# Seven block products in place of eight in the up projections of three feed-forwards

## The reference

```python
n = rmsnorm(h, P['norm_g'][l, 0]) * (1 + sc0) + s0
h = h + 0.5 * g0 * swiglu(n, P['w_ffn_up'][l, 0], P['w_ffn_down'][l, 0])
...
def swiglu(x, w_up, w_down):
    g, u = jnp.split(x @ w_up, 2, axis=-1)
    return (jax.nn.silu(g) * u) @ w_down
```

## Time and profile before

| | |
|---|---|
| timed runs, median (lowest to highest) | 3210.53 us (3208.75 to 3211.26), 3 runs |
| profiled execution, span from first to last instruction | 3212.5 us, 47873 instructions |
| TensorE matmul busy | 3108.0 us (97%), 20540 matmuls |
| VectorE busy | 1745.9 us (54%) |
| ScalarE busy | 970.0 us (30%) |
| share of the chain that ended last | PE 81%, DVE 11%, ACT 4% |
| HBM traffic | 360.24 MB read, 127 GB/s over the span |
| mean granted TensorE clock | 0.983 |

### The profile page before, as it was taken

One profiled execution on the slowest core, in us unless ns is written; L12 is line 12 of the kernel. 1 busy time (PEld: TensorE's weight loads), 2 busy tenths in 40 slices (PEclk: granted clock), 3 DMA queues, 4 the chain that ended last, 5 costly groups with the idle time before them and its releaser, 6 DMA issues.

```text
span 3212.5 us, 47873 instructions
## 1 busy us (share of the span) xinstructions
PE 3108.0 (97%) x20540; PEld 3031.3 (94%) x20540; DVE 1745.9 (54%) x2903; ACT 970.0 (30%) x1475; POOL 47.8 (1%) x92
## 2 busy tenths in 40 slices
PE   7999999998999999999999999999899999999998
PEld 4999999988999899999999999999789989999998
DVE  7656666646555655343465565664665555643334
ACT  3422312313444332121232121232244443322222
POOL 0000000000000000000000000000000000000000
PEclk9999999999999999999999999999999999999999
DMA  8255542354222523232223333334512252321221
GB/s 306 85 196 195 233 158 105 138 203 152 72 77 90 196 88 131 86 118 87 98 76 141 132 143 133 141 128 161 217 65 74 94 192 92 118 88 71 79 76 63
DMA packets 77493, 409.63 MB, mean 128 GB/s; under 512 B 8689, under 2 KB 12209, under 8 KB 46562
## 3 DMA queue, kind: packets, MB, share of 16 engines
q1 hardware_dynamic: 58656, 324.56, 27.3%
q0 software_dynamic: 9504, 56.78, 4.6%
q10 hardware_dynamic: 9122, 25.24, 2.1%
HBM read 360.24 MB, written 46.30 MB: 127 GB/s over the span
## 4 chain that ended last, share of the span: by engine, by line
PE 81%; DVE 11%; ACT 4%; issue 3%; DMA 1%; ACTq 0%; DVEq 0%
PE tile_psum L572 38%; PE tile_psum L579 20%; PE tile_psum L926 5%; PE tile_psum L533 3%; PE tile_psum L930 3%; PE misc_psum L498 3%; PE tile_psum L498 2%; PE tile_psum L538 1%; PE tile_psum L791 1%; PE tile_psum L991 1%; DVE h L1813 1%; DVE n_lo L1735 1%; DVE scaled L1718 1%; ACT squares L1250 1%; DMA raw<-in_w_proj 1%
## 5 line engine op out<-in xcount | busy, mean ns | idle before, releaser
L572 PE MATMUL tile_psum<-n_hi,whi 128*128 128x320 f32 x3264 | 744.2, 309 | 4.0 <-issue 2.1
L572 PE MATMUL tile_psum<-n_lo,whi 128*128 128x320 f32 x3264 | 741.9, 309 | 0.0
L572 PEld LDWEIGHTS tile_psum<-n_hi,whi 128*128 128x128 f32 x3264 | 546.4, 188 | 6.8 <-DVE n_lo L1735 4.2
L572 PEld LDWEIGHTS tile_psum<-n_lo,whi 128*128 128x128 f32 x3264 | 547.1, 188 | 0.0
L579 PE MATMUL tile_psum<-n_hi,wlo 128*128 128x320 f32 x3264 | 512.1, 308 | 0.0
L579 PEld LDWEIGHTS tile_psum<-n_hi,wlo 128*128 128x128 f32 x3264 | 486.9, 188 | 0.0
L1644 DVE TENSOR_TENSOR wlo<-raw,whi 128x2048 fp32r<-128x2048 f32 (+1 forms) x172 | 383.0, 2227 | 180.3 <-ACT whi L1175 178.0
L1175 ACT ACTIVATE whi<-raw 128x2048 fp32r<-128x2048 f32 (+1 forms) x172 | 319.0, 1854 | 330.1 <-DMA raw<-in_w_up 179.0
L572 PE MATMUL tile_psum<-x_hi,whi 128*128 128x320 f32 x1408 | 320.0, 309 | 0.0
L572 PE MATMUL tile_psum<-x_lo,whi 128*128 128x320 f32 x1408 | 319.6, 308 | 0.0
L1869 DVE TENSOR_TENSOR hidden<-gate_act,tile_psum 128x320 f32<-128x320 f32 x176 | 85.6, 486 | 374.9 <-ACT gate_act L1287 374.6
(11 more groups left out here) (300 smaller groups left out, 3733.9 us busy)
## 6 DMA issues: line engine op xcount, KB each, us to landing
raw<-in_w_up SPq DMA_DIRECT2D x88, 1024.0 KB, 4.8
w_ada<-in_w_ada SPq DMA_DIRECT2D x128, 512.0 KB, 5.7
raw<-in_w_down SPq DMA_DIRECT2D x32, 1024.0 KB, 4.8
raw<-in_w_gate SPq DMA_DIRECT2D x24, 1024.0 KB, 4.8
whi<-table_keep SPq DMA_DIRECT2D x20, 1024.0 KB, 4.7
wlo<-table_keep SPq DMA_DIRECT2D x20, 1024.0 KB, 7.1
g_keep<-gate_out POOLq DMA_DIRECT2D x48, 320.0 KB, 2.4
gates<-g_keep POOLq DMA_DIRECT2D x16, 960.0 KB, 5.6
```

The lines of the kernel that those rows point to most:

```text
L572: pe.matmul(tps[:, t.s, m, 0:TH], blk(p, m * n + k)[0], (hi, lo)[b][:, k, tok], start=k == 0 and b == 0, stop=False)
```

## The change

Feed-forwards 2, 3 and 4 use chunks of 4, 6, 6, 6 rows. The first chunk and all down panels are computed as before (down panels of 4 x 2 or 6 x 2 blocks). The 18 rows of the other chunks are made by a 2 x 2 block scheme with seven products. The tokens' normalised input is cut in four blocks, by token half (m) and by half of the 1024 features (k); the panel in four by gate or other half and by k. Three sums of weight blocks are new blocks, and one is replaced in place (`weight_sum`: 2 = 4 - 0, 4 = 4 - 5, 3 = 0 - 4, 6 = 1 - 3), so a panel has seven blocks of 128 x 512. Four sums of input blocks (`n_sum`) are made once in a feed-forward. Each product is 12 matmuls: 4 blocks of k, times three.

```diff
+def products(n):
+    order = []
+    for q in range(n):
+        if q == 0:
+            order += [(0, "P1"), (0, "P2"), (0, "P5"), (0, "P6"), (1, "P1"), (0, "P7")]
+        else:
+            order += [(q, "P1")] * (q > 1) + [(q, "P2"), (q - 1, "P3"), (q, "P5"), (q, "P6"), (q - 1, "P4"), (q, "P7")]
+    return order + [(n - 1, "P3"), (n - 1, "P4")]
```

These products take the place of the two calls of `pair` for each of the 18 panels. On TensorE:

```diff
+                def fast_product(q, name):
+                    g, p = g0 + q, p0 + q
+                    hi, lo, b = fast_factor(name)
+                    group = 4 * g + GROUP_OF[b] + 1
+                    pe.wait_ge(fast_hi, group)
...
+                    if name == "P1" and g >= 2:
+                        pe.wait_ge(act21, g - 1)
+                    elif name == "P2" and g >= 2:
+                        pe.wait_ge(sum11, g - 1)
+                    elif name == "P5" and g >= 2:
+                        pe.wait_ge(sum12, g - 1)
+                    elif name == "P6":
+                        pe.wait_ge(sum11, g + 1)
+                    elif name == "P7":
+                        pe.wait_ge(u2_kept, g + 1)
+                    elif name in ("P3", "P4"):
+                        pe.wait_ge(sum22, g + 1)
...
+                    for k in range(4):
+                        for x_ in (hi, lo):
+                            pe.matmul(out, blk(p, 4 * b + k)[0], x_[:, k, :], start=opens and k == 0 and x_ is hi, stop=False)
+                    pe.wait_ge(fast_lo, group)
+                    for k in range(4):
+                        ins = pe.matmul(out, blk(p, 4 * b + k)[1], hi[:, k, :], start=False, stop=k == 3)
```

`head` starts the first down tile (20 matmuls on rows 0 to n - 2) ahead of the last P3, `rest` ends it. P1, P5 and P6 are kept by ScalarE; `fast_sum11`, `fast_sum22`, `fast_sum12` on VectorE add P2, P7 and P3 to what was kept, and P4 is added in PSUM. VectorE's list:

```diff
+                for q in range(n):
+                    g = g0 + q
+                    if q:
+                        fast_sum22(g - 1)
+                        fast_low(g, 3)
+                    if q > 1:
+                        hidden_lo(q - 2)
+                    if q + 1 < n:
+                        weight_sum(g + 1, 2, 4, 0)
+                        weight_sum(g + 1, 4, 4, 5)
+                        weight_sum(g + 1, 3, 0, 4)
+                    fast_sum11(g)
+                    if q + 1 < n:
+                        weight_sum(g + 1, 6, 1, 3)
+                        fast_low(g + 1, 0)
+                    else:
+                        split_panel()
+                    if q:
+                        fast_sum12(g - 1)
+                    if q + 1 < n:
+                        fast_low(g + 1, 1)
+                        fast_low(g + 1, 2)
+                    else:
+                        split_panel()
+                    ada_step(plan[q])
+                    if q:
+                        hidden(q - 1)
```

`fast_low` makes the low parts of one of four groups of blocks, `FAST_GROUPS = [(0, 1), (2,), (5, 6), (3, 4)]`. ScalarE's list has the same groups in the same order, with the rounding of the next panel ahead of the copies of this one. The sums of the input are made in chunk 0, the first fast panel's sums among the down panels:

```diff
+                            if (i, j) == (0, 1):
+                                n_sum(0, [(h21, add, h22), (add, l21), (add, l22)])
+                            if (i, j) == (1, 1):
+                                n_sum(2, [(h21, sub, h11), (add, l21), (sub, l11)])
+                            if (i, j) == (2, 1):
+                                n_sum(1, [(sub, h11), (sub, l11)], sum_raw[0])
+                                n_sum_low(0)
+                            if (i, j) == (3, 0):
+                                n_sum_low(2)
...
+                        if c == 0 and i == 0:
+                            n_sum(3, [(h12, sub, sum_raw[1]), (add, l12)])
+                            n_sum_low(1)
+                        elif c == 0 and i == 1:
+                            n_sum_low(3)
```

In the fast chunks and their down panels `raw` and `wlo` are a ring of 17 blocks of 128 x 512 (12 old, 5 in the room of `acc`, `sq`, `tn`), `whi` a ring of 12. A fast panel takes seven places in each. It is loaded in two halves (blocks 0, 1 and 4, 5), each of which waits for the products that last used its places:

```diff
+                    for half, bs in enumerate(FAST_HALVES):
+                        for each in releases([RAW_BEFORE[p][b] for b in bs]):
+                            sp.wait_ge(*each)
...
+                        for b, r, n in raw_spans(p, bs):
+                            c0 = (2 * half + b - bs[0]) * BLK
+                            sp.dma_start(raw_at(r, n), src[:, c0:c0 + n * BLK]).then_inc(fast_in[half][g % SLOTS], 16)
```

The modulation tiles of step p - 2 still follow the load of panel p. Worked out from the ring: in the middle of a chunk the first half of panel k + 2 takes the places of P7 and P3 of panel k - 1, the second half those of P2 and P5 of panel k; the first down panel takes those of P7, P3 and P4 of the fourth fast panel. The plan of the tiles becomes (56, 36, 36, 0 in feed-forwards 1 to 4):

```diff
+ADA_PLAN = {(0, 0): [0, 0, 2, 2, 2, 2, 1, 1] + [2] * 4 + [2] * 8 + [2] * 4 + [2] * 6 + [1, 1, 0, 0],
+            (0, 1): [0, 0, 1, 1] + [1] * 4 + [1] * 6 + [2, 2, 1, 1] + [1] * 6 + [2, 2, 1, 1] + [1] * 6 + [0] * 4,
+            (1, 0): [0, 0, 1, 1] + [1] * 4 + [1] * 6 + [2, 2, 1, 1] + [1] * 6 + [2, 2, 1, 1] + [1] * 6 + [0] * 4,
+            (1, 1): [0] * len(FAST_KINDS)}
```

More of the change, by code:

```diff
@@ new lines, with before, spans @@
+RAW_AT, HI_AT = placed()
+def before(places):
+    last, out = {}, []
+    for p, at in enumerate(places):
+        out.append([last.get(pos) for pos in at])
+        last.update({pos: (p, b) for b, pos in enumerate(at)})
+    return out
+RAW_BEFORE, HI_BEFORE = before(RAW_AT), before(HI_AT)
+def spans(p, bs):
+    out = []
+    for b in bs:
+        r, h = RAW_AT[p][b], HI_AT[p][b]
+        if out and out[-1][1] + out[-1][3] == r and out[-1][2] + out[-1][3] == h and r != 4 * SLOTS:
+            out[-1][3] += 1
+        else:
+            out.append([b, r, h, 1])
+    return out
@@ new lines, in raw_spans, with arrivals @@
+def raw_spans(p, bs):
+    out = []
+    for b in bs:
+        r = RAW_AT[p][b]
+        if out and out[-1][1] + out[-1][2] == r and r != 4 * SLOTS:
+            out[-1][2] += 1
+        else:
+            out.append([b, r, 1])
+    return out
+FAST_HALVES = [(0, 1), (4, 5)]
+FAST_GROUPS = [(0, 1), (2,), (5, 6), (3, 4)]
+GROUP_OF = {b: n for n, bs in enumerate(FAST_GROUPS) for b in bs}
+def arrivals():
+    count, fast_count, out, fast_out = [0] * SLOTS, [[0] * SLOTS for _ in range(2)], [], {}
+    for p, kind in enumerate(KINDS):
+        if kind == "fast":
+            g = FAST_OF[p]
+            for half, bs in enumerate(FAST_HALVES):
+                fast_count[half][g % SLOTS] += 16 * len(raw_spans(p, bs))
+                fast_out[p, half] = fast_count[half][g % SLOTS]
+        else:
+            count[p % SLOTS] += 16 * (1 if kind == "kept" else len(raw_spans(p, range(len(RAW_AT[p])))))
+        out.append(count[p % SLOTS])
+    return out, fast_out
@@ L427, in program, with release, releases, own_wait @@
         freed = {}
+        def release(of):
+            p, b = of
+            if KINDS[p] == "prepare":
+                return table_kept[PREPARE_OF[p]], 32
+            return freed[of] if KINDS[p] == "fast" else freed[p]
+        def releases(places, but=()):
+            last = {}
+            for of in places:
+                if of is not None:
+                    s_, n_ = release(of)
+                    last[s_.name] = (s_, max(n_, last[s_.name][1]) if s_.name in last else n_)
+            for of in but:
+                if of is not None:
+                    s_, n_ = release(of)
+                    if s_.name in last and last[s_.name][1] <= n_:
+                        del last[s_.name]
+            return list(last.values())
+        def own_wait(p):
+            return [] if KINDS[p] == "kept" else releases(HI_BEFORE[p], RAW_BEFORE[p])
         class Slot:
@@ L1887, in ffn, with weight_sum @@
                 return m1
+            fast = [0]
+            def weight_sum(g, out, a, b):
+                p = PANEL_OF[g]
+                n = {2: 1, 4: 2, 3: 3, 6: 4}[out]
+                if n == 1:
+                    for half in range(2):
+                        dve.wait_ge(fast_in[half][g % SLOTS], FAST_ARRIVED[p, half])
+                if n != 2:
+                    for each in releases([RAW_BEFORE[p][out]]):
+                        dve.wait_ge(*each)
+                if n > 2:
+                    dve.wait_ge(sums_made, 4 * g + n - 1)
+                o_, a_, b_ = [raw_at(RAW_AT[p][x_]) for x_ in (out, a, b)]
+                dve.tensor_tensor(o_, a_, b_, ALU.subtract).then_inc(sums_made, 1)
```

470 lines of the change are left out of this document (418 added, 52 removed).

## The result

The changed kernel takes 3259.33 us (median of 4 runs, 3256.32 to 3264.86). The kernel before takes 3210.9 us on the same chip (3208.75 to 3211.34). The ratio is 1.0152, with an interval of 1.0137 to 1.0166. So the change costs 48 us. The forecast was 3194 and faster; the range 3140 to 3240 doesn't hold the result.

A forecast was written before the change was run, and what follows sets the result against it. TensorE, 81% of the chain, was taken as the bound. Removal, chunk 0, feed-forward 4, late tiles and fifth panels summed as -95.0 + 25 + 4 + 9.8 + 39.6 = -16.6 us; from 3210.5 that gave 3194, range 3140 to 3240.

The forecast's parts named there:

- the late tile: Feed-forwards 2 and 3: tile loads land late, costing 0.3 to 0.5 us a fast panel, 9.8 us, besides the fifth-panel waits.
- The removal: Fast panels: seven block products take 84 matmuls instead of 96, over 54 panels, saving 95.0 us.
- the products' groups: TensorE, new groups of 12 matmuls: waits within them taken as zero, with zero to 0.2 us per product possible.
- VectorE per fast panel: Fast panels with a modulation tile: VectorE needs 11.8 us against TensorE's 12.32, fitting with 4% to spare.
- C: Rival, chance 0.23: VectorE can't overlap its instructions, so a fast panel takes 13.2 us, over TensorE's 12.32; total 3234 us.
- The clock: TensorE behind each 3.9 us fifth-panel wait: 1.2 GHz for 5.5 us, 2.7 us lost, making each wait cost 6.6.
- The fifth panel: Each chunk's fifth panel, feed-forwards 2 and 3: TensorE waits 3.9 us for sum22, six times, 39.6 us with the clock.
- The end of the chunks: Chunk ends: the first down tile covers the last hidden product, cost zero; 2.7 us per chunk, 24 in all, otherwise.
- Chunk 0: Chunk 0 and its down panels: VectorE has 73.3 us of work against TensorE's 61.6; 12.5 us in each of two feed-forwards.
- Feed-forward 4: No tiles there, so VectorE's work fits; one down-panel update comes 2.0 us late, costing 4 us with the clock.
- B: Rival, chance 0.25: tile waits absent or loads landing early; 3145 us, or 3160 with half of the waits.
- A: The main case, chance 0.42: the sum of all predicted terms, -16.6 us, giving 3194 us.

The follow-up runs named there:

- the other cure: The changed kernel with the modulation tile used half a period later on VectorE, behind the next panel's sum11, load order untouched: 3175.55 us.
- all three cures: Changed kernel with tiles loaded ahead, the last down panel handled late on ScalarE and VectorE, and fewer tiles in feed-forwards 2 and 3: 3156.2 us.
- the tiles ahead: The changed kernel with the modulation tile's load issued ahead of the panel load's waits in feed-forwards 2 and 3: 3184.64 us.
- the run that mended both engines: Against the kernel with tiles ahead: ScalarE's rounding and VectorE's split of each chunk's last down panel moved behind the hidden rows' work: 3151.01 us.
- the chunks-alone kernel: The kernel before, eight products as they were, with chunks of 4, 6, 6, 6 in all feed-forwards and the changed kernel's tile plan: 3226.06 us.
- the third plan: Kernel with last down panel late, 60 tiles in feed-forward 1, 34 in each of 2 and 3, and tiles used half a period later: 3154.47 us.

## Why the prediction was wrong

It named the late tile and the right place for the longest waits, but sized the loop in the ordinary panels by the wrong path and too short a landing, and it missed a second wait. With the stages of these runs the two feed-forwards with tiles come apart. Before they took 946.3 us together. Twelve matmuls less for 36 panels are -63.4, which leaves 882.9. The changed kernel took 1020.1, so 137.2 us were given back; I get the shares by taking the cures one after the other. Each share is good to some 3 us a stage, and in another order of the cures they could differ:

| given back in feed-forwards 2 and 3 | predicted | measured | from |
|---|---|---|---|
| late modulation tile | 9.8 + 39.6 = 49.4 | 78.0 (86.0 by the other cure) | 1020.1 to 942.1; to 934.1 |
| second down panel ahead of ScalarE's kept sum | 0 | 21.8 | 942.1 to 920.3 |
| VectorE's backlog in chunk 0 and by the down panels | 25 | 33.4 | 920.3 to 886.9 |
| not explained | | 4.0 | 886.9 - 882.9 |

The last cure takes 7 of the 36 tiles out of each of the two feed-forwards; feed-forward 1, which gets them, pays 33.2 us for it. The span was forecast at -16.6 us and came out at +42.0, 58.6 off: 28.6 by the tile, 21.8 and in feed-forward 4 another 5.7 by the ends of the chunks, 8.4 by the backlog and 4.0 not explained, against 8.6 in the mixer and 1.2 elsewhere the other way.

**The removal, -95.0.** Right: panels 12.32 us apart in feed-forward 4, and with all three cures the stages are 442.7 to 444.2 us against 472.5 to 473.8, some 30 of 31.7 us. Zero for the products' groups was right too.

**VectorE per fast panel, 11.8 us.** Right: with the tiles ahead it waits 0.28 and 0.43 us a period, so it needs 11.9 to 12.0. C, given 0.23, was wrong.

**The late tile, "0.3 to 0.5 us a panel".** This is the step that failed, by its path and by its landing. The prediction closed the loop through `sum11` and P6: 5.2 + 7.8 = 13.0 us, against a period of 12.32. It asked when `sum22` was ready for P3 only where a chunk starts and at the fifth panel. By its own terms the loop from P5 over tile, `sum22`, P3 and back to P5 is 5.2 + 3.5 + 3.52 = 12.2 us, only 0.1 under the period, so any later landing is paid there, panel after panel. Measured it is 0.4 + 5.9 + 4.0 + 3.52 = 13.8 us: thirteen landings in feed-forward 2 stand in the chain, among them 6.84, 4.90 and 6.85, average 5.9 us behind the issue, so 6.3 behind P5 where 5.2 was forecast. Medians over the whole run of the kernel before, 4.8 and 5.7, were carried over to a load that now comes in pieces. In feed-forward 2 TensorE waited eleven times for `sum22` outside the fifth panels, 13.7 us, and nine times for `sum11`, 4.9 us (of which 1.8 stay with the tiles ahead). The forecast for both together was 4.9, half of 9.8.

The clock was a second error and a smaller one. The prediction charged it only at the fifth panel, while it had a row after a wait of 1.72 us, and read its 0.71 as the clock behind the wait, which was 0.57. Two of the eleven waits, 2.45 and 1.90 us, brought the clock down; behind the first it added 1.8 us inside the loop, since P3 and P5 lie on it. Periods of up to 16.6 us came out where 12.8 was forecast.

**The fifth panel, six waits of 3.9 us.** The three of feed-forward 2 were 4.79, 4.10 and 5.50 us, with a clock of 0.50 in the windows behind two of them. Place and mechanism were right and the size 0.9 short. For the first, the tile landed 6.4 us behind P4 (1344.46 to 1350.82), where 5.7 was forecast.

**The end of the chunks, "Zero; 2.7 us per chunk if that cover failed".** Wrong, but not by that cover. What I missed is a queue: on ScalarE the rounding of the second down panel stands ahead of the kept sum, and its ring place is free only when P4 of the panel before is done. Of ScalarE the prediction had asked only for its busy time, which is no bound (175 of 511 us in feed-forward 2), and not for the order of its list. P7 waited 1.75 to 2.5 us in eight of nine chunks. In feed-forward 4, without tiles, it is shown alone, here the first of three: the rounding (L1482) waits for the end of P4, then two sums are kept, then P7 starts.

```profile
2952.66 1.57 ACT L1482 ACTIVATE whi<-raw 128x1024 fp32r<-128x1024 f32 x2 [5.08 <-PE misc_psum L860]
...
2954.46 0.43 ACT L1634 ACTIVATE hidden<-misc_psum 128x320 f32<-128x320 f32 x1
...
2955.03 0.38 PE L856 MATMUL misc_psum<-n_sum_hi,whi 128*128 128x320 f32 x1 [2.47 <-ACT hidden L1634]
```

All nine were worth 33.6 us by the run that mended both engines, which is above the 24 that I had kept as a bound.

**Chunk 0, 11.7 us of waits each, 25 in all.** Near: TensorE waited 8.2 us in feed-forward 2 (2.85, 2.34, 1.99, 0.97). In the kernel with the last down panel late, 8.2 of TensorE's 12.4 us of waits for VectorE there are chunk 0's, the rest (2.44 and 1.79) stands at down panels with two tiles, where I charged nothing. If the 33.4 us divide as these waits, 22 are chunk 0's; that division is an estimate, no run separates the two.

**Feed-forward 4.** Forecast -31.7 + 4, measured -22.0; the three P7 waits (450.5 to 443.3 without them) are more than the 5.7 missing. The update of `h`, forecast 2.0 us late, was 1.18 late.

**The mixer.** The one between feed-forwards 3 and 4 took 594.6 us here and 595.7 to 601.2 in the nine others with seven products, but 603.2 before and 603.5 in the chunks-alone kernel. Its waits for `mixed` are 4.8 us (the longest 3.7 to 3.8) in the last two and 3.1 us (longest 1.7) in the changed kernel and with the tiles ahead. Why it is shorter stays open; by luck these 8.6 us bring the measured time nearer to the forecast.

**The rivals.** B had the right condition and did not happen as the code stood; the runs with the tile early or late in VectorE's list are B made true, and gave 3184.6 and 3175.6, not 3145, because of the down panel and the backlog. The chances erred in one way above all: A's own terms were taken at their middle, and no case had the tile costing more than half again what was worked out, as it did (78 to 86 us against 49.4).

## What to carry to other kernels

A transfer that is issued after a product and used ahead of the next one makes a loop. Look for every path by which it closes, not only for the one that looks longest. Compare its length with the period at the long landings, not at the median (6.5 to 6.9 us here, where the median on the row before was 5.7), and add the low clock to the loop when the waits that it makes are of a size for which a row shows that clock. Then look at each in-order list for what stands ahead of the instruction that TensorE needs: moving one line of use behind the urgent one gave 84 us here, moving one load 75, and from there two calls moved together 34, where one of them moved alone lost 8.

## What the runs showed of the hardware

Two landings in a row of the same 512 KB transfer, at the same place in SP's order, differed by 1.9 us (6.84 and 4.90). The 6.84 us one stood behind two pieces of a half panel issued 1.76 us apart (1294.36 and, in the chain above, 1296.12), the 4.90 us one behind two pieces 2.76 apart. The others in the chain of feed-forward 2, outside the fifth panels, go the same way: 6.48 to 6.85 us behind two pieces 1.76 apart (five tiles), 4.90 to 5.56 behind a wider gap or three pieces (five). Feed-forward 3 is less sharp, with one of 5.3 us among the close pairs. 1.76 us is one product at full clock, so a loop that runs without a wait makes the close pairs itself. That the gap is the cause was not tested.

```profile
1294.36 2.09 SPq L1350 DMA_DIRECT2D raw<-in_w_up  x2
1296.50 0.42 SPq L1332 DMA_DIRECT2D w_ada<-in_w_ada  x1
1309.93 0.33 SPq L1350 DMA_DIRECT2D raw_more<-in_w_up  x1
1312.69 0.33 SPq L1350 DMA_DIRECT2D raw<-in_w_up  x1
1313.07 0.42 SPq L1332 DMA_DIRECT2D w_ada<-in_w_ada  x1
```

In feed-forward 1 the time grew faster than the count of tiles: 472.6, 476.3 (478.4 in the third plan), 486.1 and 505.8 us for 56, 60, 64 and 70 tiles. A tile is 2.3 us of VectorE, so up to 60 it costs less than its own length, and from there on more. The plans differ in where the tiles stand too, and that counts: with 56 tiles, four of them on each of two steps, the chunks-alone kernel took 486.4 us there.
